# Gate row later in retention, and stick-breaking's tiles set among its heads, in a twelve-stage kernel on one core

## The reference

```python
def second_block(x, c, ...):
    for i in range(DEPTH):
        shift, scale, gate = adaln_params(c, ada_w[i, 0], ada_b[i, 0])
        h = x * (1.0 + scale) + shift
        y = stick_breaking_attention(h, ...) if i % 2 == 0 else retention(h, ...)
        x = layer_norm_2(ALPHA * x + (1.0 + gate) * y, ...)
        shift, scale, gate = adaln_params(c, ada_w[i, 1], ada_b[i, 1])
        y = grouped_moe(x * (1.0 + scale) + shift, ...)
        x = layer_norm_2(ALPHA * x + (1.0 + gate) * y, ...)
```

## Time and profile before

| | |
|---|---|
| median of 3 runs | 2008.42 us |
| profiled execution | 2009.65 us, span 2007.9 us |
| PE busy | 1768.4 us (88%) |
| DVE, ACT, POOL busy | 918.8, 653.3, 231.4 us |
| HBM read | 440.25 MB, 220 GB/s over the span |

### The profile page before, as it was taken

How to read it: one execution, slowest core, us unless ns; L and a number is a source line. 1 busy time by engine, 2 the same in 40 slices (tenths; PEclk the granted TensorE clock), 3 DMA queues, 4 the chain that set the end, 5 groups by cost and what they waited for, 6 DMA issues and landing times. The chain is left out here.

```text
span 2007.9 us, 25424 instructions
## 1 busy us (share of the span) xinstructions
PE 1768.4 (88%) x10310; PEld 1308.8 (65%) x10310; DVE 918.8 (46%) x1763; ACT 653.3 (33%) x1095; POOL 231.4 (12%) x217
## 2 busy tenths in 40 slices
PE   7988899799999979899989779989879899799884
PEld 6676786399878645699779654434478787544442
DVE  1264543366642444566545463222167665522224
ACT  1024222356631224466433731111134345311110
POOL 0000000053302021333102202000000200020000
PEclk9899899899999989899989889999989999799998
DMA  7322158344452277444426256999653445599992
GB/s 284 129 80 88 43 199 341 119 147 174 157 206 105 100 298 286 175 169 169 147 110 255 118 210 280 428 426 427 260 192 132 173 179 210 202 424 427 427 427 103
DMA packets 33562, 443.00 MB, mean 221 GB/s; under 512 B 3869, under 2 KB 4129, under 8 KB 6945
## 3 DMA queue, kind: packets, MB, share of 16 engines
q1 hardware_dynamic: 29520, 426.78, 53.1%
q0 software_dynamic: 2480, 8.92, 1.3%
q10 hardware_dynamic: 1440, 5.61, 0.7%
HBM read 440.25 MB, written 1.05 MB: 220 GB/s over the span
## 5 line engine op out<-in xcount | busy, mean ns | idle before, releaser
L82 PE MATMUL ps<-ringx,arena 128*64 128x512 f32 x1056 | 277.5, 600 | 23.6 <-DMA ringx<-in_mu 8.6
L88 ACT ACTIVATE arena<-ps 128x384 f32<-128x384 f32 (+5 forms) x233 | 101.6, 436 | 564.8 <-PE ps L82 344.0
L82 PE MATMUL ps<-xsplit_f,wsplit_f 128*128 128x256 f32 x2112 | 259.7, 286 | 17.1 <-DVE xsplit_f L91 12.3
L82 PEld LDWEIGHTS ps<-xsplit_f,wsplit_f 128*128 128x128 f32 x2112 | 257.4, 194 | 19.7 <-DVE xsplit_f L91 13.0
L82 PE MATMUL ps<-ring,arena 128*64 128x512 f32 (+1 forms) x704 | 227.2, 598 | 8.2 <-DMA ring<-in_mg 4.5
L82 PEld LDWEIGHTS ps<-ringx,arena 128*64 128x64 f32 x1056 | 91.3, 138 | 193.1 <-issue 177.2
L82 PE MATMUL ps<-xTs,ring 128*128 128x256 f32 (+1 forms) x960 | 193.1, 362 | 5.5 <-ACT xTs L88 5.5
L91 DVE TENSOR_TENSOR wsplit_f<-ring,wsplit_f 128x1024 fp32r<-128x1024 f32 x132 | 164.1, 1251 | 52.3 <-ACT wsplit_f L88 52.3
L82 PEld LDWEIGHTS ps<-xTs,ring 128*128 128x128 f32 x960 | 167.1, 199 | 28.0 <-issue 10.2
L99 DVE SCALAR_TENSOR_TENSOR arena<-ps,cp_sb,arena 128x255 f32<-128x255 f32 (+2 forms) x230 | 110.8, 482 | 130.6 <-ACT arena L88 114.1
L88 ACT ACTIVATE wsplit_f<-ring 128x1024 fp32r<-128x1024 f32 x132 | 137.5, 1051 | 51.5 <-PE ps L82 51.1
(11 more groups left out here) (175 smaller groups left out, 2454.7 us busy)
## 6 DMA issues: line engine op xcount, KB each, us to landing
ring<-in_ada SPq DMA_DIRECT2D x24, 2048.0 KB, 8.3
ring<-in_wu SPq DMA_DIRECT2D x22, 2048.0 KB, 8.0
ringx<-in_mg SPq DMA_DIRECT2D x22, 2048.0 KB, 22.1
ringx<-in_mu SPq DMA_DIRECT2D x22, 2048.0 KB, 24.9
ringx<-in_md SPq DMA_DIRECT2D x22, 2048.0 KB, 25.7
ring<-in_md SPq DMA_DIRECT2D x12, 2048.0 KB, 27.4
ring<-in_mg SPq DMA_DIRECT2D x12, 2048.0 KB, 22.1
ring<-in_mu SPq DMA_DIRECT2D x12, 2048.0 KB, 25.9
```

What stands on the lines that cost most here:

```text
L82: return self.e.matmul(o, l, r, start=start, stop=stop, skip_group_check=True)
L88: return self.e.activation(o, i, f, **k)
```

## The change

In the delta rule convolution 12 stands ahead of the first pair of `L2`, and DVE writes the columns of units 1 to 3 between convolutions. Step 0 of all four units stands in a row, then convolutions 18 and 19, then the other steps; DVE's four products `LT` follow the four additions. At the end three sums of 512 columns take the place of six of 256, and the output product begins with row tile 6, which needs no norm, then the sums, then tile 7, then the rest; so it needs the second matrix of `woe` first.

In stick-breaking the matrix's columns are laid out anew: each load holds two tiles of q and the two of k of the same heads. The first block of rows of v and one tile stand ahead, eleven tiles, the second block and the gate row are fillings among the heads' steps. POOL's passes over the residual (`rows_applied`) stand in filling 6. The heads' outputs have their own buffer.

In retention the gate row stands in the output product, ahead of its chunk 10. All heads get only the multiplication by the norm in their last step; the multiplications by the gate of heads 0 to 3 stand in fillings 4 to 7, ACT rounds, DVE subtracts one filling later. `wro`'s last matrix is asked for ahead of two expert matrices.

All narrow loads are issued as two halves of 1 MB, each with its own semaphore, and each waits only for the chunks that lie in its half.

```diff
 SWA = weave(8, 4, 3, 12)
-L2 = weave(6, 2, 3, 6)
-GDN = weave(4, 17, 4, 6 + ADA)
+L2 = [(None, 0)] + [(u, k if u is not None else k + 1) for u, k in weave(6, 2, 3, 5)]
+
+GDN = [(u, 0) for u in range(4)] + [(None, 0), (None, 1)] \
+    + [(u, k + 1 if u is not None else k + 2) for u, k in weave(4, 16, 4, 4 + ADA)]
-SBU = weave(16, 3, 4)
+
+SB_FILL = [[("T", 1, 1)], [("T", 1, 2)], [("T", 1, 3)], [("T", 2, 0)], [("T", 2, 1)], [("T", 2, 2), ("T", 2, 3)], [("R", 5, 0)],
+           [("T", 3, 0), ("T", 3, 1)], [("T", 3, 2), ("T", 3, 3)]]
+SBU = weave(16, 3, 4, len(SB_FILL))
+UPPER = (4, 5, 6, 7)
 GATES = [("vr", 2)] + [("g", i) for i in range(8, 12)] + [("vr", 3)] + [("g", i) for i in range(12, 16)]
 RETU = weave(8, 3, 3, len(GATES))
+
+GATED = {4: (0, 1), 5: (2, 3, 4, 5), 6: (6,), 7: (7,)}
...
-SB_CH = chunks("T", *[("ws", j) for j in range(1, 4)]) + chunks("R", ("ws", 4), ("ws", 5)) + chunks("D", ("wso", 0), ("wso", 1))
+
+SB_CH = chunks("R", ("ws", 4)) + chunks("T", ("ws", 1), ("ws", 2)) + chunks("R", ("ws", 5)) + chunks("T", ("ws", 3)) \
+    + chunks("D", ("wso", 0), ("wso", 1))
...
-    out += [("ws", j) for j in range(6)] + one[:3] + [("wso", 0), ("wso", 1)] + one[3:]
+    out += [("ws", j) for j in (0, 4, 1, 2, 5, 3)] + one[:3] + [("wso", 0), ("wso", 1)] + one[3:]
     out += [("wr", j) for j in range(6)] + [("wrv", 0), ("wrv", 1), ("wrv", 2), ("wr", 6), ("wrv", 3), ("wr", 7)]
-    out += two[:2] + [("wro", j) for j in range(3)] + two[2:4] + [("wro", 3)] + two[4:]
+    out += two[:2] + [("wro", j) for j in range(4)] + two[2:]
     return out
 
...
-            for n in range(6):
+
+            banks = [bank(("dn", 0), i) for i in range(4)]
+
+            def block(k, h):
+                view = slot(("woe", k // 4), 4)
+                for c in range(2):
+                    r = mm(banks[2 * h + c], E.oT[:, k, h * 128:h * 128 + 128], view[:, k % 4, c * 512:c * 512 + 512],
+                           k == 6, k == 5)
+                return r
+
+            t.wait_ge(*arrived(("woe", 1)))
+            t.wait_ge(*a("swo"))
+            for h in range(2):
+                block(6, h)
+            for n in range(3):
                 t.wait_ge(*a("rms_sq", n))
-                rms_sums(("rms", n), E.tmp3[n][:, 0:256])
+                rms_sums(("rms", n), E.sq[n])
             t.note("early", 0)
-            t.wait_ge(*v("rms", 5))
-            t.wait_ge(*a("swo"))
-            down([("woe", 0), ("woe", 1)], ("dn", 0), E.oT)
+            for h in range(2):
+                block(7, h)
+            t.wait_ge(*arrived(("woe", 0)))
+            t.wait_ge(*v("rms", 0))
+            for k, h in ((0, 0), (0, 1), (1, 0), (1, 1)):
+                block(k, h)
+            for h in range(2):
+                for k in range(2, 6):
+                    t.wait_ge(*v("rms", k // 2))
+                    r = block(k, h)
+                r.then_inc(s_pe, t.did("dn", 0, "half", h))
+            for j in range(2):
+                t.note("used", ("woe", j))
             t.note("pre", 0)
...
-            for i in range(12):
-                tile_split(4, i, "ps", 4 + i)
-            for j in range(2):
-                rows_split(4, 12 + 4 * j, f"vs{j}")
-            gate_row(0, B.gk, v)
+            rows_split(4, 0, "vs0")
+            tile_split(4, 4, "ps", 4)
             for u, k in SBU:
+                if u is None:
+                    for kind, j, c in SB_FILL[k]:
+                        if kind == "T":
+                            tile_split(4, CHUNKS[4].index((("ws", j), "T", c)), "ps", 4 * j + c, UPPER)
+                        else:
+                            gate_row(0, B.gk, v, UPPER)
+                            rows_split(4, 12, "vs1", UPPER)
+                    continue
...
-            down_split(4, ("dn", 4), 20, lambda f: xth[:, f, :], lambda f: B.olo[:, f, :], lambda f: v("sbo", 2 * f + 1))
+            down_split(4, ("dn", 4), 20, lambda f: B.ohi[:, f, :], lambda f: B.olo[:, f, :], lambda f: v("sbo", 2 * f + 1))
...
-            gate_row(2, Q.gk, v)
...
-                       lambda f: v("gsplit", f))
+                       lambda f: v("gsplit", f), {10: lambda: gate_row(2, Q.gk, v)})
...
                 if u is None:
                     conv(12 + k)
+                    if 2 <= k < 5:
+                        gdn_columns(k - 1)
...
             v.wait_ge(*a("l2", 5))
+            gdn_columns(0)
             for u, k in GDN:
                 if u is None:
+                    if k == 0:
+                        for i in range(4):
+                            v.wait_ge(*a("gdDT", i))
+                            v.wait_ge(*t("gdb", i))
+                            tt(E.u[i]["LT"], E.u[i]["DT"], ps("gdb", i)[:, 0:384], ALU.mult).then_inc(s_dve, v.did("free", "gdb", i))
                     ada_piece(0, k - 6)
                 else:
                     gdn(u, k)
...
+                if c < 2:
+                    n = 4 * j + c
                     v.wait_ge(*t("ps", n))
-                    ts(B.qk[:, n, :], ps("ps", n)[:, 0:256], 0.125, None, ALU.mult).then_inc(s_dve, v.did("free", "ps", n))
+                    ts(B.qk[:, 2 * j + c, :], ps("ps", n)[:, 0:256], 0.125, None, ALU.mult).then_inc(s_dve, v.did("free", "ps", n))
                     v.note("ps", n)
-                if n >= 3:
-                    low_half(4, n)
+
+            for c in range(2):
+                q_tile(0, c)
+            for i in range(3, 8):
+                low_half(4, i)
             for h in range(2):
                 evac_rows("vs0", h, B.vs[:, h, 0:512])
-            gate_row(0, B.gk)
+            q_tile(1, 0)
+            i = 8
             for u, k in SBU:
-                if k == 0:
+                if u is None:
+                    if k == 6:
+                        gate_evacuated(0)
+                    for kind, j, c in SB_FILL[k]:
+                        for _ in range(1 if kind == "T" else 4):
+                            low_half(4, i)
+                            i += 1
+                        if kind == "T":
+                            q_tile(j, c)
+                    if k == 5:
+                        gate_columns(0, B.gk)
+                elif k == 0:
...
                 elif k == 2:
                     base, n = (u % 2) * 64, u // 2
                     v.wait_ge(*t("sbo", u))
-                    o, hi = ps("sbo", u)[base:base + 64, 0:256], xth[base:base + 64, n, :]
+                    o, hi = ps("sbo", u)[base:base + 64, 0:256], B.ohi[base:base + 64, n, :]
...
-            for i in range(24, 28):
+            while i < 28:
                 low_half(4, i)
+                i += 1
             norm(4, lambda i: ps(("dn", 4), i), True)
...
-            def gated(u, d, o):
-                g_ = Q.gT[:, 2 * u + d, :]
-                stt(g_, o, C("rgn", 2 * u + d, 2 * u + d + 1), g_, ALU.mult, ALU.mult).then_inc(s_dve, v.did("rout", u))
-                v.note("gated", 2 * u + d)
-
-            def gated_low(u, d):
-                f = 2 * u + d
+
+            def gated(f):
+                u, d, g_ = f // 2, f % 2, Q.gT[:, f, :]
+                if u >= 4:
+                    v.wait_ge(*a("gT", 8 if u < 6 else 12))
+                stt(g_, Q.qk[:, u + 8 * d, :], C("rgn", f, f + 1), g_, ALU.mult, ALU.mult).then_inc(s_dve, v.did("gated", f))
+
+            def gated_low(f):
+                u, d = f // 2, f % 2
+                v.wait_ge(*a("ghi", f))
                 tt(Q.glo[:, f, :], Q.gT[:, f, :], Q.ghi[:, u + 8 * d, :].bitcast(F32), ALU.subtract) \
                     .then_inc(s_dve, v.did("gsplit", f))
 
...
+                    for f in GATED.get(k - 1, ()):
+                        gated_low(f)
+                    for f in GATED.get(k, ()):
+                        gated(f)
...
                     for d in range(2):
-                        od = o[:, d * 256:d * 256 + 256]
-                        if u < 4:
-                            tt(od, od, w[:, 0:256], ALU.mult).then_inc(s_dve, v.did())
-                            v.wait_ge(*a("gT", 2 * u + d))
-                            gated(u, d, od)
-                            copy(Q.ghi[:, u + 8 * d, :], Q.gT[:, 2 * u + d, :]).then_inc(s_dve, v.did())
-                            gated_low(u, d)
-                        else:
-                            tt(Q.qk[:, u + 8 * d, :], od, w[:, 0:256], ALU.mult).then_inc(s_dve, v.did("unit", u))
+                        tt(Q.qk[:, u + 8 * d, :], o[:, d * 256:d * 256 + 256], w[:, 0:256], ALU.mult).then_inc(s_dve, v.did("unit", u))
             for f in range(16):
                 low_half(6, i + f + 3)
+                if 0 < f < 9:
+                    gated_low(7 + f)
                 if f < 8:
-                    u, d = 4 + f // 2, f % 2
-                    v.wait_ge(*a("gT", 8 if u < 6 else 12))
-                    gated(u, d, Q.qk[:, u + 8 * d, :])
-                if 0 < f < 9:
-                    v.wait_ge(*a("ghi", 7 + f))
-                    gated_low(4 + (f - 1) // 2, (f - 1) % 2)
```

(27 more changed lines are left out.)

164 lines of the change are left out of this document (93 added, 71 removed).

## The result

The changed kernel takes 1961.67 us, the median of 4 runs (1960.83 to 1966.77). The kernel before took 2008.45 us beside it. The ratio is 0.9769, with a 95% interval from 0.9749 to 0.9790. That is faster by 46.8 us, where 58.4 us were forecast. The profiled execution took 1961.27 us with a span of 1959.5 us, 48.4 us less than the span before.

A forecast was written before the change was run, and what follows sets the result against it. PE was taken as the bound, gains lying where it waits or runs slow. Gains 3.2 + 14.2 + 13.9 + 10 + 17.3 = 58.6 us off 2009.65, less 1.2 to the median: 1950 us; own range 1942 to 1957, wide 1934 to 1968.

The forecast's parts named there:

- the heads don't overlap: Rival in stick-breaking: engines working in order keep heads and fillings apart, gain 0 to -3 us, 1960 to 1963 us; chance 0.12.
- Parts 1 to 3: First stage: normalisation of q and k, opening the delta-rule units, end of stage; gains 3.2, 14.2 and 13.9 us.
- The normalisation: First stage, q and k: a convolution ahead of the first sums covers PE's wait for ACT; gain 3.2 us.
- The opening: Delta-rule units: 24 products in a row replace unit-by-unit chains, 28.5 us becoming 14.3; gain 14.2 us.
- The end: End of first stage: rows needing no norm replace serial rounds, 46.3 us becoming 32.4; gain 13.9 us.
- Part 4: Stick-breaking: fillings among the heads cover waits for POOL's masks, 108.5 us becoming 98.5; gain 10 us, bounds -3 and 20.
- heads' 30 us: Stick-breaking: the heads' 36.04 us of PE work hold about 6 us lost to lower clock, so 30 at full.
- "Free" for the halved loads: Narrow loads: two halves cost at most 9.6 us, beside 11 us in which PE uses the other slot.
- Part 5: Retention: waits for gate row, DVE's chain and last matrix go, with less slow clock; gain 17.3 us, bounds 9 and 21.
- The serial chain comes back: Rival: DVE becomes the bound behind the opened units and in retention, 6 and 8 us less, 1964 us; chance 0.11.
- The lock's price: Rival in stick-breaking's sixth filling: halves and masks queue behind POOL's passes, 8.8 us for 1.4, 1957 us; chance 0.08.
- The halved loads would have to cost: Slower rival: halved loads stall PE at all 24 matrices of two stages; at 14 us each, 2017 us; chance 0.02.

The follow-up runs named there:

- experiment 10: Changed kernel with the first stage's lists of normalisations and of the delta rule as before; 1985.12 us, one execution.
- experiment 6: Changed kernel with the four banks of stick-breaking's output product taken from banks 0 to 3; 1962.48 us, one execution.
- experiments 1 to 3: Changed kernel, retention's output product: ACT's rounding one chunk later plus DVE's old order, 1949.78 us; ACT's part alone, 1950.95 us; DVE's alone, 1955.56 us.
- experiments 7 and 8: Changed kernel with all stick-breaking fillings issued ahead of the heads, 1977.64 us; with POOL's passes over the residual behind the heads, 1965.69 us.
- Experiments 1 and 4: Changed kernel, retention's output product: ACT's rounding one chunk later and DVE's old order, 1949.78 us; copy of gate row's columns moved to chunk 1, 1952.56 us.
- experiment 8: Changed kernel with POOL's four passes over the residual moved behind stick-breaking's heads; 1965.69 us, one execution.

## Why the prediction was right, and where not

**The total.** 1961.67 us is 11.7 us above the forecast and outside its own range of 1942 to 1957, though inside the wide one. It lies among the times of the rivals: 1960 to 1963 us was to mean that the heads don't overlap, and by their stage they do (8.2 us of 10). The total alone would have named the wrong cause. That the unchanged parts add up to almost nothing is luck: 3.3 us gained in one place against 3.6 lost in three.

**Parts 1 to 3** stood. The normalisation gave 3.0 us (forecast 3.2): 39.2 us from the convolution at 157.2 to the end of the convolutions, now 36.2. The opening gave 28.5 - (17.1 - 3.5) = 14.9 (14.2). The end gave 16.0 (13.9): the load was in time by about 0.1 us, where 1 us of wait was counted, and there was no slow clock. In experiment 10, with less time for it, the same load was waited for 2.9 us.

**Part 4** had the size right (8.2 for 10) and one wait missing, and this was partly luck: up to the output product the waits come to 9.8 us where 10.2 were counted, because the masks cost less. What is over is PE's own work, 90.2 us busy against 88.3, so the heads' 30 us "at full" clock were too low by about 2. Masks cost 5.8 us against 8.7, the rest 1.2 against 1.5; the bank that the last head holds took 2.8 us that no step of the sum contained (experiment 6). The passes of POOL were counted at 1.4 us and cost 1.0. "Free" for the halved loads was right for the change, but too modest: without them, the weave loses 7.3 us.

**Part 5** is the step that failed, in one sentence: the gate row's work inside the down product "free", by counting that PE has three split chunks while DVE makes three copies. The count left out what the columns stand behind, a DVE that follows ACT in a ring of 3.64 us a chunk against 2.8. Its price was 6.1 us of wait, 1.7 us for `ringlo` and 2.7 us of slow clock, 10.5 of the 11.4 us that the stage lost (experiments 1 to 3). With the ring mended, the stage gains 18.3 us, and the forecast for it was 17.3. The 2.9 us wait behind the last rows was as forecast.

**The rivals.** "The serial chain comes back" is what happened in retention, with 11.4 us for 8; in the opening it did not. The argument against it, 75.88 busy us of 125.9, was no argument: of a turn's 3.64 us DVE is busy 2.15 and ACT 1.46. The lock's price and the slow heads are out (experiments 7 and 8). The halved loads would have to cost; they gain.

Sum: 58.6 - 10.4 (part 5: the ring's 11.4, less 1.0 by which the rest did better) - 1.8 (part 4) + 2.2 (parts 1 to 3) - 0.3 (unchanged stages) = 48.3. The spans differ by 48.4.

## What to carry to other kernels

Busy shares can't show a ring. When two engines hand a tile to and fro in one loop, add up one turn, waits included, and compare it with what the third engine needs for a step. Letting the consumer take the tile of the step before (one line here) opens the ring. A copy moved "beside" other work stands behind all that its engine has queued there. Where a stage ends, ask who still holds the banks that the next product takes; and when you give it others, look where the turn puts the next stage's banks, since the wait may only move.

## What was not expected of the hardware

After a wait of 6.5 us PE ran the next 21.5 us at a mean clock of 0.86, with no idle time in them; after one of 0.4 us it stayed at 1.00. The low clock lies at the start of the 21.5 us, and from 1646 us on it is 1.00:

```profile
1639.60:1643.00 3.40, 3.40 (x16) 3.40 (x17) 0.69 (x1) 0.00 (x0) 0.00 (x0) 0.50 0.00 0
1643.00:1646.00 3.00, 3.00 (x10) 2.43 (x10) 1.82 (x2) 0.00 (x0) 0.00 (x0) 0.59 0.00 0
```

That is 2.7 us for the same work (21.5 and 18.8), near half of what the wait itself cost. Experiments 1 and 4 gained 3.6 and 2.7 us more than the waits they took away, and in 1 the clock is 2.7 us of it. Not every wait did this: behind the 2.8 us ahead of stick-breaking's output product the clock stayed at 1.00.

And five halves of DVE beside four passes of POOL took 13.8 us instead of 6.1, while the passes took 12.4. POOL in experiment 8, where only two halves stood beside the passes:

```profile
1112.07 10.58 POOL L91 TENSOR_TENSOR xs<-xs,lnp 128x1024 f32<-128x1024 f32 x4
```

That is 10.6 us for the four, 2.65 each where it was 3.1 with five halves.
